# Modulation rows summed on VectorE, tables loaded behind the first weights, and two scores ahead of a norm

## The chip, the cores and the metric

The kernel runs on one core of one Trainium2 chip, in one launch. The metric is device microseconds of one execution; what is given for a kernel is the median of several runs.

## The reference

Two transformer-like blocks are computed one after the other, all in float32, for 512 tokens ("latent") and, in the first block, 256 context tokens beside them. What the change touches is this part of the first block (depth 2) and the attention of the second:

```python
for l in range(DEPTH):                                   # DEPTH = 2
    mod_l = jax.nn.silu(c) @ w_ada[l] + b_ada[l]         # w_ada: 1024 x 3072; c is one row
    sh_l, sc_l, gt_l = jnp.split(mod_l[:, None, :], 3, axis=-1)
    mod_c = jax.nn.silu(c_ctx) @ w_ada[l] + b_ada[l]     # the same for the context
    ...
    h_l = _rmsnorm(x, g_pre[l]) * (1.0 + sc_l) + sh_l
    pl = _split_proj(h_l @ w_in[l])                      # short conv, attention, gated linear attention
    ...
    x = x + gt_l * _rmsnorm(out_l, g_post[l])
# second block
bq = rms_norm(bq.reshape(B, S, B_HEADS, HEAD_DIM_2), gains[2])
cq = rms_norm(cq.reshape(B, S, C_HEADS, HEAD_DIM_2), gains[4])
oa = diff_attention(aq, ak, av, lam, bias_a)             # heads A, B and C
ob = banded_attention(bq, bk, bv, bias_b, B_WINDOW, sinks[layer])
oc = nsa_attention(cq, kc, vc, ksel, ckv[:, :, 3], kwin, ...)
```

A modulation row is a product of a vector of 1024 with a matrix: the two vectors silu(c) and silu(c_ctx) against each 128 columns of `w_ada`.

## The kernel before, in words

Every engine has its own instruction stream, written out by hand in the order in which it works; the streams meet at semaphores and, at the end of each phase, at a barrier (`phase_end`) that all of PE, ACT and DVE pass.

**A tile** is a weight block of 1024 x 128 floats (512 KB) in one of the four slots of `ring`. SP loads it in two DMAs of 256 KB (`load`, L638), in the order of use and not before the slot is free (`w_used`). POOL splits it in two halves of rounded numbers, `whi` and `ring_parts`, with two instructions of 128x1024 (`split`, L859 and L861). PE then multiplies (`turned_tile`, three matmuls for each of eight 128-row pieces and each stretch of tokens) into one of two PSUM pairs, used in turn; a pair is free again when ACT or DVE has read it (`pair_free`).

**The phases** are: load, ada0, then for each layer attn, branch1, gla, branch2, conv, branch0, and for the second block kv2, cmp, heads, branches2, up, down, end.

**Load and ada0.** SP issues the constants (`con`, 3008 KB in one DMA: identity, ones, two more matrices and a rotation in the first 640 columns; then cosines, sines and the tables of the linear attention), x (2048 KB), ctx (1024 KB) and 24 small rows (L643). PE, POOL and the rest wait until all have landed (`inputs_in`). PE transposes x, ACT copies it out, the phase ends; SP then writes x to DRAM (`keep_x`) and goes on with `w_ada`. In ada0 PE computes the squares' sums and then 16 modulation tiles of layer 0 as matmuls with 2 moving columns. The first four are loaded ahead.

**conv0** is the convolution phase of layer 0. It has eight iterations; one is four tiles of 768 tokens, in the order z, c, x, b. ACT takes the tanh of z (`z_tanh`) and copies c; DVE multiplies tanh and z (that frees the pair for x), multiplies c and x (frees it for the next z), runs seven instructions of the convolution on SBUF (L2402 and L2055) and multiplies with b. Between the tiles lie the 32 modulation tiles that are still needed (8 of layer 0, 24 of layer 1): SP loads one beside each ring tile into `mod_ring` (`load_mod`, L707), and PE, behind each of the four tiles, multiplies it in 8 matmuls with 2 moving columns. Each such fp32 matmul stands twice in the trace. DVE copies the 8 numbers of an iteration to `mods` (L2417).

**heads** starts with four query tiles, each followed by a norm (ACT squares, PE sums with `block_norm_mm`, ACT takes the root, DVE multiplies in `normed_query`). Then PE runs `scores`, with DVE's `maximum` (L2553), ACT's exp and DVE's `normalise` behind, 96 heads' pieces long. PE issues `all_read`, one small matmul for the gates, and waits for the fourth norm before the first score; ACT's fourth norm stands ahead of its first exp.

Of the kernel before, what the change touches and what calls it, by code (L numbers as in the profile page):

```python
# [22 lines left out]
P = 128  # L23
# [198 lines left out]
def two_blocks(nc, a, out, stop=None):  # L222
    ctx = ExitStack()
    with ctx:
# [3 lines left out]
        def sem(name):  # L228
            return ctx.enter_context(nc.semaphore(name))
# [49 lines left out]
        def take(*shape, at=None):  # L279

            n = int(np.prod(shape))
            o = used[0] if at is None else at
            used[0] = o + n
            assert used[0] <= FREE, (shape, used[0], FREE)
            v = arena[:, o:o + n]
            if len(shape) == 2:
                v = v.rearrange("p (a b) -> p a b", a=shape[0])
            if len(shape) == 3:
                v = v.rearrange("p (a b c) -> p a b c", a=shape[0], b=shape[1])
            return v  # L290
# [26 lines left out]

        mod_ring = take(4, KT, P, at=used[0] - KT * ALL)
        gin = arena[:, base:base + 4 * ALL].rearrange("p (s n) -> p s n", s=4)
# [137 lines left out]
        h_ready, h_scaled, h_hi, h_lo = sem("h_ready"), sem("h_scaled"), sem("h_hi"), sem("h_lo")  # L457
        mod_landed, mod_used = [sem(f"mod_landed{s}") for s in range(4)], sem("mod_used")
        x_kept, x_back, x_new = [sem(f"x_kept{h}") for h in range(2)], sem("x_back"), sem("x_new")
        pair_free = [sem(f"pair_free{s}") for s in range(2)]  # L460

        phase, inputs_in, out_done = sem("phase"), sem("inputs_in"), sem("out_done")
        act_own, dve_own = sem("act_own"), sem("dve_own")
        x_turned, par_turned = sem("x_turned"), sem("par_turned")
# [163 lines left out]
        def _(sp):  # L628
# [15 lines left out]

            sp.dma_start(con[:], a["con"]).then_inc(inputs_in, 16)
            sp.dma_start(y_in[:, 0:LT, :], a["x"][0].rearrange("(t p) f -> p t f", p=P)).then_inc(inputs_in, 16)
# [43 lines left out]
            for l in range(DEPTH):  # L690
                w = a["w_in"][l]
                n = ALL if l == 0 else LAT
                if l == 0:

                    for s in range(4):
                        load(a["w_ada"][0][:, s * P:(s + 1) * P])
                    sp.wait_ge(phase, 3 * phases_to("load"))
                    keep_x(ALL)
                    with sp.Fori(0, 3) as i, tiles.loop(i, 3, 4):
                        for s in range(4):  # L700
                            load(a["w_ada"][0][:, ds(i * 512 + (4 + s) * P, P)])
# [7 lines left out]
                def conv(i, mods_of=None):  # L709

                    for s, c in enumerate((CZ, CC, CX, CB)):
                        load(w[:, i * P + c:i * P + c + P] if isinstance(i, int) else w[:, ds(i * P + c, P)])
                        if mods_of:

                            if not isinstance(i, int) or i > 0:
                                sp.wait_ge(mod_used, i * 4 + (s - 3))
                            else:
                                sp.wait_ge(phase, 3 * phases_to("branch2_0"))
                            load_mod(s, mods_of(s))
# [43 lines left out]
                if l == 0:  # L763

                    for i in range(2):
                        conv(i, lambda s: a["w_ada"][0][:, (16 + 4 * i + s) * P:(17 + 4 * i + s) * P])
                    with sp.Fori(0, 6) as i, tiles.loop(i, 6, 4):
                        conv(i + 2, lambda s: a["w_ada"][1][:, ds(i * 512 + s * P, P)])
                else:
                    with sp.Fori(0, KT) as i, tiles.loop(i, KT, 4):  # L770
                        conv(i)
# [127 lines left out]
        def _(pe):  # L899
# [143 lines left out]
            for l in range(DEPTH):  # L1043
# [20 lines left out]

                def conv(i, cond):
                    for s in range(4):
                        turned_tile(hP, n)
                        if cond is None:
                            continue

                        pe.wait_ge(mod_landed[s], i * 32 + 32)
                        if s == 0:
                            pe.wait_ge(mod_read, i)
                        for k in range(KT):
                            last = mm(bank(6)[:, 2 * s:2 * s + 2], mod_ring[:, s, k], cond[:, :, k], k == 0, k == KT - 1)
                        last.then_inc(mod_used, 1)

# [226 lines left out]
                if phase_end(f"branch2_{l}"):  # L1304
                    return
                if l == 0:
                    with pe.Fori(0, 2) as i, tiles.loop(i, 2, 4), uses.loop(i, 2, 4), splits.loop(i, 2, 4):
                        conv(i, conds[0])
                    with pe.Fori(0, 6) as i, tiles.loop(i, 6, 4), uses.loop(i, 6, 4), splits.loop(i, 6, 4):
                        conv(i + 2, conds[1])  # L1310
                else:
                    with pe.Fori(0, KT) as i, tiles.loop(i, KT, 4), uses.loop(i, KT, 4), splits.loop(i, KT, 4):
                        conv(i, None)
                if phase_end(f"conv{l}"):
# [68 lines left out]
            for c in range(4):  # L1383
                turned_tile(hP, LAT)
                if c:
                    block_norm_mm(NORM0 + c - 1, blk)
            block_norm_mm(NORM0 + 3, blk)
            all_read()
            fill_steps = [0]
# [78 lines left out]
            mm(bank(1, 96), anti, gates.rearrange("p t m -> p (t m)"), True, True).then_inc(gates_turned, 1)  # L1468
            pe.wait_ge(n2_ready, NORM0 + 4)
            for n in range(3):  # L1470
                scores(n)
            for n in range(4 * NS2 + 3):
# [569 lines left out]
        def _(dve):  # L2042
# [79 lines left out]
            for l in range(DEPTH):  # L2122
# [52 lines left out]
                def rotated_tile(c, dst):  # L2175
                    dve.wait_ge(rot_read, c + 1)
                    dve.wait_ge(qn_ready, c + 1)
                    v.tensor_tensor(dst[:, 0:LAT], rope_t, rope_s, ALU.add).then_inc(q_ready, 1)

                nb = NORMED * l  # L2180
                qg, kg = par[l][:, R_QG:R_QG + 1], par[l][:, R_KG:R_KG + 1]
# [199 lines left out]
                ns = len(stretches)  # L2381
                with dve.Fori(0, KT) as i, tiles.loop(i, KT, 4), uses.loop(i, KT, 4), own.loop(i, KT, 4 * ns):
                    p = product()
                    dve.wait_ge(z_tanh, i + KT * l + 1)
                    last_read()
                    stt(tmp[:, 0:n], tha[:, 0:n], 1.0, pair(p, n), ALU.add, ALU.mult).then_inc(pair_free[p], 1)
                    skip()
                    last_read()
# [25 lines left out]
                    if l == 0:  # L2414

                        dve.wait_ge(mod_used, i * 4 + 4)
                        v.tensor_copy(mods[:, ds(i * 4 + 16, 4)], bank(6, 8).rearrange("p (a b) -> p a b", a=4)).then_inc(mod_read, 1)  # L2417
# [114 lines left out]
            own(v.tensor_scalar(nsink, sinkb, -1.0, None, ALU.mult))  # L2532
            for c, g in enumerate((0, 1, 2, 4)):
                normed_query(NORM0 + c, qt_[:, 0, c], gain(g), c)
# [57 lines left out]
            maximum(0)  # L2592
            maximum(1)
            for n in range(4 * NS2):
                i, m = divmod(n, NS2)
# [95 lines left out]
```

## Time and profile before

| | |
|---|---|
| median of 3 runs | 4250.06 us (4243.55 to 4252.66) |
| the profiled execution | 4246.85 us; span of the trace 4245.0 us |
| PE | 3942.7 us busy, 93% of the span, mean granted clock 0.955 |
| POOL | 1945.0 us, 46% |
| DVE | 1675.9 us, 39% |
| ACT | 974.7 us, 23% |
| DMA | 305.21 MB, mean 72 GB/s |

Times are microseconds from the start of the span. An engine's idle time costs something only if the work that ends last waits for it. A matmul's own duration overlaps with the next one's, so the distance from start to start is what counts.

### The profile page before, as it was taken

To read this page: it belongs to the slowest core of one execution; us is meant where nothing else is said; L and a number is where in the kernel's file an instruction comes from. 1 tells how busy PE (TensorE), PEld (TensorE's weight loads), DVE (VectorE), ACT (ScalarE), POOL (GpSimd) and SP (SyncE) were. 2 spreads that over 40 slices of the span, in tenths; PEclk is the share of its full clock that TensorE was granted. 3 is DMA by queue.
4 is the path that set the end of the run, shared out by engine and by line. 5 is a ranking of instruction groups with operands and counts; after the bars stand their busy time and mean duration, and the time that the engine had idled before them with its cause. 6 is when DMAs were issued, how large, how long until landed. Compare 5 with 4: busy or idle time off the path is not lost. (4 is left out here: it accounts for less than half of the span.)

```text
span 4245.0 us, 52930 instructions
## 1 busy us (share of the span) xinstructions
PE 3942.7 (93%) x20171; PEld 3147.9 (74%) x20171; DVE 1675.9 (39%) x2552; ACT 974.7 (23%) x1729; POOL 1945.0 (46%) x834
## 2 busy tenths in 40 slices
PE   6999999999989998899999998899888998999999
PEld 5777788888878897676678777677585544877877
DVE  1444317556631224244426555445303555132200
ACT  2333312222210001334312222110213444102200
POOL 1333243332335444344453433587452220886886
PEclk7899999999999998999999999999888998999999
DMA  6111221111226543222231221334432110343333
GB/s 189 41 46 46 61 68 46 47 43 46 52 64 127 106 89 109 70 48 60 56 82 49 60 55 45 82 93 100 120 90 55 33 35 8 92 106 79 94 92 91
DMA packets 512284, 305.21 MB, mean 72 GB/s; under 512 B 37769, under 2 KB 492818, under 8 KB 511210
## 3 DMA queue, kind: packets, MB, share of 16 engines
q1 hardware_dynamic: 500010, 282.43, 27.3%
q10 hardware_dynamic: 12096, 20.33, 1.4%
q8 instruction: 122, 2.00, 0.2%
q14 instruction: 56, 0.46, 0.0%
HBM read 276.42 MB, written 26.27 MB: 71 GB/s over the span
## 5 line engine op out<-in xcount | busy, mean ns | idle before, releaser
L859 POOL TENSOR_TENSOR whi<-ring,con 128x1024 fp32r<-128x1024 f32 (+1 forms) x415 | 967.4, 2331 | 2245.1 <-DMA ring<-in_w_in 1740.0
L548 PE MATMUL ps<-xT_parts,whi 128*128 128x512 f32 (+2 forms) x2632 | 1009.9, 384 | 63.0 <-DVE hT_parts L2093 35.7
L548 PE MATMUL ps<-hT_parts,whi 128*128 128x512 f32 (+1 forms) x2864 | 1049.8, 367 | 0.0
L861 POOL TENSOR_TENSOR ring_parts<-ring,whi 128x1024 fp32r<-128x1024 f32 (+1 forms) x415 | 979.5, 2360 | 32.5
L548 PE MATMUL ps<-xT_parts,ring_parts 128*128 128x512 f32 (+2 forms) x2600 | 945.6, 364 | 0.0
L548 PE MATMUL ps<-arena_parts,whi 128*128 128x512 f32 (+1 forms) x2472 | 767.7, 383 | 68.7 <-DVE arena_parts L2087 57.8
L1544 ACT ACTIVATE arena<-ps 128x512 f32<-128x512 f32 (+7 forms) x583 | 311.4, 544 | 1685.6 <-PE ps L548 975.1
L548 PE MATMUL ps<-arena 128*128 128x128 f32 (+9 forms) x3292 | 646.0, 341 | 27.6 <-DVE arena L2055 21.9
L548 PEld LDWEIGHTS ps<-xT_parts,whi 128*128 128x128 f32 (+1 forms) x2632 | 501.0, 190 | 170.2 <-issue 66.1
L548 PEld LDWEIGHTS ps<-hT_parts,whi 128*128 128x128 f32 x2864 | 544.9, 190 | 90.8 <-issue 7.0
L548 PEld LDWEIGHTS ps<-arena_parts,whi 128*128 128x128 f32 x2472 | 460.2, 194 | 177.2 <-issue 66.3
L548 PEld LDWEIGHTS ps<-arena 128*128 128x128 f32 (+3 forms) x3292 | 438.4, 194 | 180.5 <-issue 122.1
L548 PEld LDWEIGHTS ps<-xT_parts,ring_parts 128*128 128x128 f32 (+1 forms) x2600 | 492.9, 190 | 84.5 <-issue 0.8
L548 PE MATMUL ps<-arena_parts,ring_parts 128*128 128x512 f32 (+1 forms) x1440 | 549.5, 382 | 0.0
L2055 DVE SCALAR_TENSOR_TENSOR arena<-arena,ps 128x256 f32<-128x256 f32 (+2 forms) x200 | 127.6, 638 | 553.4 <-PE ps L548 417.8
L548 PEld LDWEIGHTS ps<-arena_parts,ring_parts 128*128 128x128 f32 x1440 | 278.9, 194 | 52.0
L548 PE MATMUL ps<-arena,con 128*128 128x512 f32 (+5 forms) x626 | 227.0, 501 | 29.2 <-ACT arena L1544 28.7
L548 PE MATMUL ps<-whi,xT_parts 128*128 128x256 f32 (+2 forms) x640 | 190.0, 297 | 10.8 <-ACT arena L1544 7.3
L548 PE MATMUL ps<-whi,hT_parts 128*128 128x256 f32 (+2 forms) x640 | 184.0, 287 | 0.0
L548 PE MATMUL ps<-ring_parts,xT_parts 128*128 128x256 f32 (+2 forms) x640 | 183.5, 287 | 0.0
L548 PEld LDWEIGHTS ps<-arena,con 128*128 128x128 f32 (+1 forms) x626 | 99.2, 177 | 109.2 <-issue 59.6
L2055 DVE SCALAR_TENSOR_TENSOR arena<-arena,par 128x512 f32<-128x512 f32 (+2 forms) x83 | 103.3, 1252 | 192.3 <-ACT arena L1544 185.7
(158 smaller groups left out, 3388.2 us busy)
## 6 DMA issues: line engine op xcount, KB each, us to landing
ring<-in_w_in SPq DMA_DIRECT2D x504, 256.0 KB, 3.9
arena<-in_w_ada SPq DMA_DIRECT2D x64, 256.0 KB, 4.8
ring<-in_w_up SPq DMA_DIRECT2D x64, 256.0 KB, 4.0
ring<-in_w_down SPq DMA_DIRECT2D x64, 256.0 KB, 3.9
ring<-in_w_out SPq DMA_DIRECT2D x48, 256.0 KB, 3.8
gates_kept<-stage ACTq DMA_DIRECT2D x24, 384.0 KB, 3.9
arena<-gates_kept SPq DMA_DIRECT2D x24, 384.0 KB, 3.7
ring<-in_w_ada SPq DMA_DIRECT2D x32, 256.0 KB, 4.0
```

The source lines that it names most:

```text
L548: return nc.tensor.matmul(o, l, r, start=first, stop=last)
L859: v.tensor_tensor(hi, raw, ones[:, 0:m].unsqueeze(1).to_broadcast([P, kt, m]), ALU.mult).then_inc(w_rounded, 1)
L861: v.tensor_tensor(ringR[:, s, 0:kt, 0:m], raw, hi.bitcast(F32), ALU.subtract).then_inc(w_split, 1)
L1544: return nc.scalar.activation(o, i, f, **kw)
L2055: return v.scalar_tensor_tensor(out=o, in0=a0, scalar=s, in1=a1, op0=op0, op1=op1)
```

## The change

There are three parts.

**Modulation rows in conv0.** A slot of `mod_ring` now holds 256 rows by 512 columns of `w_ada` (two pieces of 128 rows; runs of 2 KB in DRAM, before 512 bytes) and the four slots hold all 1024 rows. DVE weighs: for each of the eight pieces k and each of the two vectors c it multiplies the piece with the vector's numbers, one per partition, and adds it to `mod_sum[:, c]` (128x512): 16 instructions in an iteration, eight ahead of the product of z and eight behind it, with a wait for the own last ones ahead of each k. Then it raises `mod_summed`. PE sums over the partitions with ones as the moving operand: 8 matmuls with one column in an iteration, behind tile b, instead of 32. SP waits for `mod_summed` of the iteration before ahead of every slot, where before it waited for PE's use of that slot. `conds[1]`, which holds the same numbers as `conds[0]`, serves both layers.

**Constants in two DMAs.** The first 640 columns go first as before; the rest (5376 columns, 2688 KB) goes behind the first four tiles of `w_ada`, and ahead of SP's wait for the phase and of `keep_x`. DVE waits for it (`tables_in`) ahead of its first use.

**Heads.** PE issues the gates' matmul and the first two scores behind the third norm's matmul, then `all_read`, the fourth norm's matmul, the third score, and a wait for the fourth root. DVE takes the gates and the first two maxima ahead of the fourth `normed_query`.

```diff
-        mod_ring = take(4, KT, P, at=used[0] - KT * ALL)
+        mod_ring = take(4, 2, 512, at=used[0] - KT * ALL)
+        mod_sum = take(2, 512)
+        used[0] += KT * ALL - 5 * 1024
...
-            sp.dma_start(con[:], a["con"]).then_inc(inputs_in, 16)
+            first_con = C_AT["cos"][0]
+            sp.dma_start(con[:, 0:first_con], a["con"][:, 0:first_con]).then_inc(inputs_in, 16)
...
                     for s in range(4):
                         load(a["w_ada"][0][:, s * P:(s + 1) * P])
+                    sp.dma_start(con[:, first_con:], a["con"][:, first_con:]).then_inc(tables_in, 16)
                     sp.wait_ge(phase, 3 * phases_to("load"))
                     keep_x(ALL)
...
                             if not isinstance(i, int) or i > 0:
-                                sp.wait_ge(mod_used, i * 4 + (s - 3))
+                                sp.wait_ge(mod_summed, i)
...
-                        conv(i, lambda s: a["w_ada"][0][:, (16 + 4 * i + s) * P:(17 + 4 * i + s) * P])
+                        conv(i, lambda s: a["w_ada"][0][256 * s:256 * s + 256, (16 + 4 * i) * P:(20 + 4 * i) * P])
...
-                def conv(i, cond):
+                def conv(i, with_mods):
                     for s in range(4):
                         turned_tile(hP, n)
-                        if cond is None:
-                            continue
-
-                        pe.wait_ge(mod_landed[s], i * 32 + 32)
-                        if s == 0:
+                        if s == 3 and with_mods:
+                            pe.wait_ge(mod_summed, i + 1)
                             pe.wait_ge(mod_read, i)
-                        for k in range(KT):
-                            last = mm(bank(6)[:, 2 * s:2 * s + 2], mod_ring[:, s, k], cond[:, :, k], k == 0, k == KT - 1)
-                        last.then_inc(mod_used, 1)
+                            for m in range(4):
+                                for c in range(2):
+                                    last = mm(bank(6)[:, 2 * m + c:2 * m + c + 1], mod_sum[:, c, m * P:(m + 1) * P],
+                                              ones[:, 0:1], True, True)
+                            last.then_inc(mod_used, 1)
...
-            block_norm_mm(NORM0 + 3, blk)
-            all_read()
...
-            pe.wait_ge(n2_ready, NORM0 + 4)
-            for n in range(3):
-                scores(n)
+            scores(0)
+            scores(1)
+            all_read()
+            block_norm_mm(NORM0 + 3, blk)
+            scores(2)
+            pe.wait_ge(rs2_ready, NORM0 + 4)
...
+                dve.wait_ge(tables_in, 16)
...
+                def weigh_mods(i, ks):
+
+                    for k in ks:
+                        if k % 2 == 0:
+                            dve.wait_ge(mod_landed[k // 2], i * 32 + 32)
+                        own.settle()
+                        for c in range(2):
+                            m_, c_ = mod_ring[:, k // 2, k % 2], conds[1][:, c, k:k + 1]
+                            if k == 0:
+                                own(v.tensor_scalar(mod_sum[:, c], m_, c_, None, ALU.mult))
+                            else:
+                                own(stt(mod_sum[:, c], m_, c_, mod_sum[:, c], ALU.mult, ALU.add))
+
+                with dve.Fori(0, KT) as i, tiles.loop(i, KT, 4), uses.loop(i, KT, 4), own.loop(i, KT, 4 * ns + 16 * (l == 0)):
+                    if l == 0:
+                        weigh_mods(i, range(4))
                     p = product()
                     dve.wait_ge(z_tanh, i + KT * l + 1)
                     last_read()
                     stt(tmp[:, 0:n], tha[:, 0:n], 1.0, pair(p, n), ALU.add, ALU.mult).then_inc(pair_free[p], 1)
+                    if l == 0:
+                        weigh_mods(i, range(4, KT))
+                        own.settle()
+                        v.memset(stat[:, 3, 6:7], 0.0).then_inc(mod_summed, 1)
...
-                        dve.wait_ge(mod_used, i * 4 + 4)
+                        dve.wait_ge(mod_used, i + 1)
...
-            for c, g in enumerate((0, 1, 2, 4)):
+            for c, g in enumerate((0, 1, 2)):
                 normed_query(NORM0 + c, qt_[:, 0, c], gain(g), c)
...
             maximum(0)
             maximum(1)
+            normed_query(NORM0 + 3, qt_[:, 0, 3], gain(4), 3)
```

## Rows read from the trace of the kernel before

**Rows 1.** The page, part 1: busy time, share of the span, instructions.
```profile
PE 3942.7 (93%) x20171; PEld 3147.9 (74%) x20171; DVE 1675.9 (39%) x2552; ACT 974.7 (23%) x1729; POOL 1945.0 (46%) x834
```

**Rows 2.** Busy time by stretch, conv0: us, busy (count) of each, clock, DMA.
```profile
1360.00:1400.00 40.00, 40.00 (x255) 35.93 (x254) 7.46 (x12) 2.90 (x3) 19.30 (x8) 1.00 0.50 101
```

**Rows 3.** Timeline of PE, start of conv0: start, us, operation, count, idle before.
```profile
1274.56 0.49 PE L548 MATMUL ps<-xT_parts,whi 128*128 128x512 f32 x1 [2.36 <-DVEq L2049]
...
1276.17 0.63 PE L548 MATMUL ps<-xT_parts,whi 128*128 128x512 f32 x1
...
1284.59 1.84 PE L548 MATMUL ps<-small,arena 128*128 128x2 f32 x16
1286.93 0.49 PE L548 MATMUL ps<-xT_parts,whi 128*128 128x512 f32 x1 [0.50 <-POOL ring_parts L861]
...
1295.44 1.84 PE L548 MATMUL ps<-small,arena 128*128 128x2 f32 x16
1297.14 0.48 PE L548 MATMUL ps<-xT_parts,whi 128*128 128x512 f32 x1
```

**Rows 4.** Timeline of DVE, conv0, the third iteration and the fourth's first product.
```profile
1369.07 0.95 DVE L2055 SCALAR_TENSOR_TENSOR arena<-arena,ps 128x768 f32<-128x768 f32 x1 [10.51 <-ACT arena L1544]
1387.16 1.15 DVE L2393 TENSOR_TENSOR arena<-arena,ps 128x512 f32<-128x512 f32 x2 [17.14 <-PE ps L548]
1388.46 0.49 DVE L2402 TENSOR_SCALAR arena<-arena,par 128x512 f32<-128x512 f32 x1 [0.15 <-DVE arena L2393]
1389.11 0.75 DVE L2055 SCALAR_TENSOR_TENSOR arena<-arena,par 128x512 f32<-128x512 f32 x1 [0.16 <-DVE arena L2402]
1390.01 0.75 DVE L2055 SCALAR_TENSOR_TENSOR arena<-arena,par 128x512 f32<-128x512 f32 x1 [0.15 <-DVE arena L2055]
1390.80 0.35 DVE L2402 TENSOR_SCALAR arena<-arena,par 128x256 f32<-128x256 f32 x1
...
1392.23 0.96 DVE L2055 SCALAR_TENSOR_TENSOR arena<-arena 128x768 f32<-128x768 f32 x1
...
1409.71 0.95 DVE L2055 SCALAR_TENSOR_TENSOR arena<-arena,ps 128x768 f32<-128x768 f32 x1 [10.51 <-ACT arena L1544]
```

**Rows 5.** Timeline of DVE, conv0, the convolution's last instruction one iteration later.
```profile
1432.86 3.13 DVE L2055 SCALAR_TENSOR_TENSOR arena<-arena 128x768 f32<-128x768 f32 x1
```

**Rows 6.** Timeline of POOL, the same moment.
```profile
1432.78 2.40 POOL L859 TENSOR_TENSOR whi<-ring,con 128x1024 fp32r<-128x1024 f32 x1 [5.31 <-DMA ring<-in_w_in]
1435.26 2.99 POOL L861 TENSOR_TENSOR ring_parts<-ring,whi 128x1024 fp32r<-128x1024 f32 x1
```

**Rows 7.** Timeline of DVE, the same convolution in layer 1, where POOL hardly rests.
```profile
2754.47 2.65 DVE L2055 SCALAR_TENSOR_TENSOR arena<-arena,par 128x512 f32<-128x512 f32 x1 [0.16 <-DVE arena L2402]
2757.63 2.38 DVE L2055 SCALAR_TENSOR_TENSOR arena<-arena,par 128x512 f32<-128x512 f32 x1 [0.51 <-DVE arena L2055]
```

**Rows 8.** Timeline of SP's queue, conv0: the issue of one ring tile.
```profile
1326.28 1.42 SPq L638 DMA_DIRECT2D ring<-in_w_in  x2
```

**Rows 9.** Timeline of POOL, the start on that tile.
```profile
1331.28 2.41 POOL L859 TENSOR_TENSOR whi<-ring,con 128x1024 fp32r<-128x1024 f32 x1 [5.63 <-DMA ring<-in_w_in]
```

**Rows 10.** Timeline of the start: SP's last small row and PE's first work.
```profile
12.73 0.34 SPq L643 DMA_DIRECT2D arena<-in_norm_mlp  x1
...
22.87 0.85 PE L1022 MATMUL ps<-con,arena 108*128 108x108 f32 x3 [22.87 <-DMA arena<-in_norm_mlp]
```

**Rows 11.** Busy time by stretch: the first loads, and ada0 behind its third tile.
```profile
0.00:22.80 22.80, 0.00 (x0) 0.00 (x0) 0.09 (x2) 1.28 (x1) 0.20 (x4) 1.00 0.96 318
...
50.50:60.00 9.50, 9.50 (x46) 9.50 (x46) 0.48 (x3) 0.00 (x0) 0.00 (x0) 0.50 1.02 205
```

**Rows 12.** Timeline of DVE, ada0: the copies behind the third and the fourth tile.
```profile
50.62 0.16 DVE L2141 COPY mods<-ps 128x2 f32 x1 [1.63 <-PE ps L548]
53.89 0.16 DVE L2141 COPY mods<-ps 128x2 f32 x1 [3.12 <-PE ps L548]
```

**Rows 13.** Timelines of PE, DVE and ACT at the first scores.
```profile
3229.07 1.13 PE L548 MATMUL ps<-arena,con 128*128 128x512 f32 x2 [1.93 <-ACT arena L1544]
...
3233.93 1.72 PE L548 MATMUL ps<-arena 64*128 64x128 f32 x8 [2.63 <-DVE arena L2055]
...
3232.00 1.88 DVE L2055 SCALAR_TENSOR_TENSOR arena<-arena,par 128x512 f32<-128x512 f32 x1 [1.90 <-ACT arena L1544]
...
3230.13 0.60 ACT L1544 ACTIVATE arena<-ps 128x512 f32<-128x512 f32 x1 [1.11 <-DVE arena L2055]
```

More of the change, by code:

```diff
@@ L458, in two_blocks @@
         mod_landed, mod_used = [sem(f"mod_landed{s}") for s in range(4)], sem("mod_used")
+        mod_summed = sem("mod_summed")
         x_kept, x_back, x_new = [sem(f"x_kept{h}") for h in range(2)], sem("x_back"), sem("x_new")
@@ L462, in two_blocks @@
         phase, inputs_in, out_done = sem("phase"), sem("inputs_in"), sem("out_done")
+        tables_in = sem("tables_in")
         act_own, dve_own = sem("act_own"), sem("dve_own")
@@ L765, in _ @@
                     for i in range(2):
-                        conv(i, lambda s: a["w_ada"][0][:, (16 + 4 * i + s) * P:(17 + 4 * i + s) * P])
+                        conv(i, lambda s: a["w_ada"][0][256 * s:256 * s + 256, (16 + 4 * i) * P:(20 + 4 * i) * P])
                     with sp.Fori(0, 6) as i, tiles.loop(i, 6, 4):
-                        conv(i + 2, lambda s: a["w_ada"][1][:, ds(i * 512 + s * P, P)])
+                        conv(i + 2, lambda s: a["w_ada"][1][256 * s:256 * s + 256, ds(i * 512, 512)])
                 else:
@@ L1305, in _ @@
                     return
[L1306 to L1313, printed above, removed]
+                with pe.Fori(0, KT) as i, tiles.loop(i, KT, 4), uses.loop(i, KT, 4), splits.loop(i, KT, 4):
+                    conv(i, l == 0)
                 if phase_end(f"conv{l}"):
@@ L2381, in _ @@
                 ns = len(stretches)
-                with dve.Fori(0, KT) as i, tiles.loop(i, KT, 4), uses.loop(i, KT, 4), own.loop(i, KT, 4 * ns):
+                def weigh_mods(i, ks):
[12 more added lines that the diff above has]
+                        weigh_mods(i, range(4))
                     p = product()
```

## Prediction

> **What bounds the kernel now.** I read the page first: PE is busy 93% of the span, POOL 46%, DVE 39% [rows 1], so time is won where PE gets less to do or waits less, and lost where another engine takes over. Then the busy time by stretch for the stages that the change touches. In conv0 PE is busy 40.00 of 40 us at full clock, while POOL works 19.30 us and DVE 7.46 [rows 2]: PE sets the pace there, and DVE looks nearly empty. The timelines tell the rest. On PE's, the 16 records (8 matmuls) of a modulation tile hold the next tile back from 1295.44 to 1297.14, so 1.70 us [rows 3]. On DVE's, the product of z comes every 40.64 us (1369.07 to 1409.71), the length of an iteration [rows 4]. An iteration is four tiles and four times 1.70, so a bare tile is (40.64 - 6.80) / 4 = 8.46 us. At the start nothing computes for 22.87 us until the inputs have landed, with the DMA engines 0.96 busy at 318 GB/s [rows 10, 11]. At the first scores PE waits 2.63 us for DVE's fourth norm [rows 13].
>
> **Part 1, conv0, what PE saves.** 32 matmuls with 2 columns become 8 with one: three of four stretches of 1.70 us go, 5.10 us an iteration. The trace has no one-column matmul; its nearest row is the two-column one, whose length is set by loading weights, so I take 1.70 for eight of them (from 1.5 to 2.0). If PE stays the pace, an iteration is 35.54 us and eight save 40.8 us.
>
> **What DVE gets.** 16 instructions of 128x512 with all operands in SBUF. With POOL silent such a one starts 0.79 us after the one before it (1390.01 to 1390.80), or 0.90 with the wait for its own result (1389.11 to 1390.01) [rows 4]. Two per k: 1.69 us, less for k = 0, so 6.3 us for the eight ahead of z's product and 6.8 for the eight behind. That is 13 us beside some 9 us of old work: by busy time alone it fits into 35.5 us easily.
>
> **Why it fits badly.** DVE's instructions on SBUF and POOL's splits exclude each other. The convolution's last instruction takes 0.96 us with POOL silent [rows 4] and 3.13 when it starts just after a split [rows 5]: it ends 0.81 us after that split does, and the next split grows from 2.40 to 2.99 [rows 6]. In layer 1, where POOL hardly rests, the 0.75 us instruction takes 2.65 and 2.38, one per split [rows 7]. So each split that meets a stream of such instructions costs the stream 1.6 to 2.2 us (2.65 - 0.75 = 1.90, 3.13 - 0.96 = 2.17), at most a whole split, 2.4 [rows 6]; I take 2.1. Products that read PSUM are not held up: 0.95 each time [rows 4].
>
> The Trainium skill, SBUF — State Buffer, "Who interferes with whom", has this as a rule that speaks against the change: a VectorE instruction with two SBUF inputs and a GpSimd instruction that reads SBUF shut each other out for the whole instruction, whichever starts first. The rows agree with it (3.13 against 0.96). By that rule at its hardest, each meeting costing a whole split of 2.40 us, the loop worked out next would be 23.1 + 8 x 2.40 = 42.3 us, against the 38.9 that I take.
>
> **The loop that closes on DVE.** The pair that z used must be freed before tile x may start. From z's product to the next one: tile x 8.46; product c times x 1.30; seven instructions of the convolution 4.73 (1388.46 to 1393.19) [rows 4]; b's product and the copy about 1.3; the eight weighings ahead of z 6.3; z's product 1.0. Sum 23.1 us without POOL. The second eight weighings lie under tile x.
>
> POOL adds eight splits an iteration. How many fall into the 15 exposed instructions? SP decides. Its mod slots, and behind them the ring tiles c, x and b, now wait for `mod_summed`, which comes only near the end of tile x. A ring tile reaches POOL 5.0 us after issue (1326.28 to 1331.28) [rows 8, 9]. So c and x are split when the convolution runs, b and the next z during the first weighings: nearly all eight splits hit the exposed stream. Seven give 23.1 + 14.7 = 37.8 us, eight give 39.9. I take the middle, 38.9. Tile x then waits for 38.9 - 35.5 = 3.4 us, and such a pause costs clock: behind the 2.36 us pause at 1274.56 matmuls come at half clock from 1276.17 on, seven of them at twice the distance, some 1.4 us [rows 3]. Taken in about a third of the iterations: 39.3 us. Bounds: 35.5 (no meeting that matters) and 23.1 + 8 x 2.4 + 1.4 = 43.7.
>
> So conv0 gains 8 x (40.64 - 39.3) = 10.7 us. At the end the last convolution, stretched by three splits (4.73 + 6.3 + 1.3 against a tile b of 8.46), ends late by 3.9 us less what overlaps: I take 3 back. **Net 8 us** (from +40 gained to 27 lost).
>
> What else moves there: the new mod DMAs have runs of 2 KB. The 512-byte runs go at 205 GB/s with the DMA engines full, the start's long ones at 318 [rows 11]; 4 MB in 39 us needs 108 GB/s either way, so this is nothing on the path. PE's new wait for `mod_summed` stands behind tile b, 8 us after the sum is made; behind it are queued only the sums and the next z. SP's wait holds back three ring tiles, by up to 7 us of the 25 us lead that four slots give: it costs nothing itself except that it bunches the splits.
>
> **Part 2, the constants.** Ahead of the first work 6080 KB become 3392. At 318 GB/s this takes 11 us instead of 19.6. But SP issues its last small row only at 12.73 [rows 10], and small ones need some 2 us to land: start at about 15.2 instead of 22.87, 7.7 us earlier. What is late next: SP's queue. Behind the four `w_ada` tiles (2 MB at 205 GB/s [rows 11], until 24) come 2688 KB of tables (until 32.5), then `keep_x`'s 3 MB (until 42), and only then the fifth tile, here at about 46. PE's third tile ends at 50.6 before, so at 42.9 now, and a tile takes 1.8 us there (1.63 idle and 0.16 between DVE's copies) [rows 12]: it would want the fifth tile at 44.7. Behind it the clock is 0.50 and a tile takes 3.4 us, twice 1.70, slower than DMA's 2.6 (512 KB at 205 GB/s) [rows 11], so nothing more is lost. 1.3 us back, rounded: **6.5 us gained** (3 to 8; if the row issue went faster, too).
>
> **Part 3, the heads.** The first scores leave the 2.63 us wait behind [rows 13], but `all_read` now stands ahead of the fourth norm's matmul and waits for ACT's copy that ends at 3230.73, where the matmul had started at 3229.07: the fourth root, and ACT's first exp queued behind it, come 1.6 us later. Maxima 0 and 1 are saved on DVE. I take 0.5 us gained, from 1.5 gained to 1.5 lost, the loss if the norm meets a split once more.
>
> **Sum.** 8 + 6.5 + 0.5 = 15 us off the profiled execution, 4246.85 - 15 = 4231.9. It lies 3.2 us under the median shown, so the forecast for a median is 4235.
>
> **Rivals.**
> A, the forecast: DVE and POOL in turn set conv0's pace, 38 to 40.3 us; 4235 (4228 to 4244).
> B, PE keeps the pace: the loads land so that most splits fall under tile x or where DVE waits for PE, 35.5 to 37.5 us an iteration. For it: DVE's busy time is small [rows 2]; against it: SP's order. 25 to 40 us in conv0, 4203 to 4218, middle 4211.
> C, slower: all eight splits meet the exposed stream at 2.2 to 2.4 us and the clock falls at each pause. It loses in all from 41.1 us an iteration on, since the two other parts' 7 us less 3 at the end are then used up; at 42.6 us it is 15.7 + 3 - 7 = 12 us slower, 4262.
> D, the start gives nothing: the tables only push `keep_x` and the fifth tile, and PE waits there for what it had won; conv0 as in A. 4241. The DMA row (0.96 busy) speaks for it; that the copies from the third tile on come 3.3 us apart [rows 12], more than DMA's 2.6 for a tile, against it.
>
> **Chances.** A 0.56, B 0.20, C 0.14, D 0.10. A measurement of this kernel tells about 0.2%, 8.5 us, from no change. A is beyond that in four of five cases (0.45), D in less than half (0.04), B always: faster 0.69. C lies beyond it with 0.08, the rest is the same, 0.23. For the range I leave out the lower half of B and the upper half of C: 4212 to 4255.
>
> **What would show it.** In the changed trace: PE's records of 128x1 in eight places, 1.7 us each; z's product every 39 us (B: 35.5; C: over 41); weighings of 0.75 us beside ones of 2.4 to 2.7, one per split; a pause of PE ahead of tile x put down to DVE, and the clock under 1.00 in conv0, where it was 1.00; PE's first matmul at 15 us; ada0's fifth tile late by about 1 us and all that follows ada0 some 6 us earlier. Wrong would be the forecast if weighings that meet splits don't stretch, if the splits fall elsewhere, or if the fifth tile of `w_ada` waits long.

## The result

The changed kernel takes 4226.6 us (median of 13 runs, 4210.3 to 4240.5) where the kernel before takes 4251.3 us (13 runs, 4243.6 to 4268.3) beside it. The ratio is 0.9938, 95% interval 0.9922 to 0.9953: 20 to 33 us faster. The profiled execution of after has a span of 4225.5 us, 19.5 less than before's.

The page of after, part 1, to be laid beside [rows 1]:

```profile
PE 3915.8 (93%) x19787; PEld 3111.2 (74%) x19787; DVE 1858.1 (44%) x2688; ACT 975.5 (23%) x1729; POOL 1958.6 (46%) x834
```

PE has 384 records fewer (8 iterations, 24 matmuls, two records each) and DVE 136 instructions more: 8 times 16 weighings and a memset.

**conv0.** Busy time by stretch of after (the columns of [rows 2]), around its second and third iteration:

```profile
1300.00:1340.00 40.00, 33.21 (x189) 28.97 (x188) 35.71 (x32) 2.91 (x3) 21.12 (x8) 0.91 0.56 112
1340.00:1380.00 40.00, 40.00 (x236) 35.15 (x235) 35.52 (x34) 2.91 (x3) 20.69 (x8) 1.00 0.54 114
```

DVE, 7.46 us in [rows 2], is busy for 35.5 of 40. PE has lost 6.79 us of the first stretch and nothing of the second. The timeline of after's DVE, from one product of z (1286.67) over the next (1330.34) to the third (1365.06):

```profile
1286.67 0.94 DVE L2055 SCALAR_TENSOR_TENSOR arena<-arena,ps 128x768 f32<-128x768 f32 x1
1287.54 13.37 DVE L2055 SCALAR_TENSOR_TENSOR arena<-arena,cond 128x512 f32<-128x512 f32 x8
...
1301.13 1.15 DVE L2413 TENSOR_TENSOR arena<-arena,ps 128x512 f32<-128x512 f32 x2
...
1306.20 0.96 DVE L2055 SCALAR_TENSOR_TENSOR arena<-arena 128x768 f32<-128x768 f32 x1
...
1308.48 5.20 DVE L2392 TENSOR_SCALAR arena<-arena,cond 128x512 f32<-128x512 f32 x2
1313.71 16.71 DVE L2055 SCALAR_TENSOR_TENSOR arena<-arena,cond 128x512 f32<-128x512 f32 x6
1330.34 0.94 DVE L2055 SCALAR_TENSOR_TENSOR arena<-arena,ps 128x768 f32<-128x768 f32 x1
1331.21 5.75 DVE L2055 SCALAR_TENSOR_TENSOR arena<-arena,cond 128x512 f32<-128x512 f32 x8
1337.03 0.06 DVE L2406 MEMSET stat<- 128x1 f32 x1
1341.49 1.15 DVE L2413 TENSOR_TENSOR arena<-arena,ps 128x512 f32<-128x512 f32 x2 [4.40 <-PE ps L552]
...
1345.13 2.38 DVE L2422 TENSOR_SCALAR arena<-arena,par 128x256 f32<-128x256 f32 x1
...
1352.66 3.04 DVE L2055 SCALAR_TENSOR_TENSOR arena<-arena 128x768 f32<-128x768 f32 x1
...
1356.80 4.00 DVE L2392 TENSOR_SCALAR arena<-arena,cond 128x512 f32<-128x512 f32 x2
1360.83 4.32 DVE L2055 SCALAR_TENSOR_TENSOR arena<-arena,cond 128x512 f32<-128x512 f32 x6
1365.06 0.95 DVE L2055 SCALAR_TENSOR_TENSOR arena<-arena,ps 128x768 f32<-128x768 f32 x1
```

And POOL's at the same time, the first and the last of eight splits without a rest, and the next one:

```profile
1308.44 2.41 POOL L865 TENSOR_TENSOR whi<-ring,con 128x1024 fp32r<-128x1024 f32 x1 [10.98 <-DMA ring<-in_w_in]
...
1327.20 2.67 POOL L867 TENSOR_TENSOR ring_parts<-ring,whi 128x1024 fp32r<-128x1024 f32 x1
1344.58 2.79 POOL L865 TENSOR_TENSOR whi<-ring,con 128x1024 fp32r<-128x1024 f32 x1 [14.71 <-DMA ring<-in_w_in]
```

The first iteration lasts 43.67 us, the second 34.72. In the first all eight splits meet the eight weighings ahead of z: 5.20 + 16.71 = 21.9 us, where the same number with POOL silent (1331.21) takes 5.75, so 2.0 us per split. Four more splits had met the weighings behind z before (13.37 instead of 5.75 us), so that the product of c and x came 14.46 us after z's: twelve splits met in one interval. In the second POOL rests until the convolution has begun; the eight weighings behind z stand untouched, DVE waits 4.40 us for PE, and six splits meet what it has to do until z. Long iterations don't follow each other: the intervals between products of z are 43.67, 34.72, 36.02, 40.19, 34.97, 38.10, 36.09, mean 37.7, where before each was 40.64. What PE sees of it, timeline and waits of after in conv0 (for the waits: us in total, times, longest):

```profile
1305.94 1.84 PE L552 MATMUL ps<-con,arena 128*128 128x1 f32 x16
1307.64 0.47 PE L552 MATMUL ps<-xT_parts,whi 128*128 128x512 f32 x1
...
1331.43 0.77 PE L552 MATMUL ps<-xT_parts,whi 128*128 128x512 f32 x1 [6.79 <-DVE arena L2055]
```
```profile
PE ps L552 <- DVE arena L2055: 11.5, 4, 6.8
```

From DVE's first instruction in conv0 to the last copy of modulation numbers the phase takes 305.5 us, before 327.9: 22.4 us less.

**The start.** SP's last small row and PE's first work, after's answer to [rows 10]:

```profile
10.32 0.29 SPq L647 DMA_DIRECT2D arena<-in_norm_mlp  x1
...
16.38 0.85 PE L1028 MATMUL ps<-con,arena 108*128 108x108 f32 x3 [16.38 <-DMA arena<-in_norm_mlp]
```

PE starts 6.49 us earlier. DVE's copies of ada0, which answer to [rows 12], follow each other as before: the fourth comes 3.24 us behind the third (3.27 there), and the fifth 3.42 behind the fourth (57.31 - 53.89 = 3.42 there), so the fifth tile isn't late:

```profile
44.14 0.16 DVE L2141 COPY mods<-ps 128x2 f32 x1 [1.63 <-PE ps L552]
47.38 0.16 DVE L2141 COPY mods<-ps 128x2 f32 x1 [3.09 <-PE ps L552]
50.80 0.16 DVE L2141 COPY mods<-ps 128x2 f32 x1 [3.25 <-PE ps L552]
```

**Where the rest went.** At the start of conv0 after is 6.2 us ahead of before, at its end 28.6, at the first product of branch0 31.2, at the first norm of heads 30.5 (3215.74 against 3185.27), at the 51st of DVE's 160 maxima there 29.9, at the 121st 29.2, at the last only 19.4. Those last 10 us are lost in one place. Busy time by stretch, after from 3512 on and then before at the same point of its work, 29 us later (the column behind POOL's is the granted clock):

```profile
3512.00:3522.00 10.00, 9.67 (x22) 4.04 (x21) 5.33 (x19) 5.47 (x18) 0.00 (x0) 0.50 0.01 2
3522.00:3532.00 10.00, 10.00 (x30) 5.58 (x28) 2.37 (x8) 2.11 (x6) 0.00 (x0) 0.50 0.00 0
3532.00:3542.00 10.00, 9.86 (x33) 6.50 (x32) 5.95 (x28) 4.47 (x18) 0.00 (x0) 0.50 0.00 1
```
```profile
3541.00:3551.00 10.00, 9.10 (x40) 4.67 (x40) 7.20 (x27) 6.96 (x24) 0.00 (x0) 1.00 0.00 1
3551.00:3561.00 10.00, 8.81 (x45) 5.53 (x44) 6.96 (x32) 5.50 (x21) 0.00 (x0) 0.92 0.01 2
3561.00:3571.00 10.00, 10.00 (x19) 3.09 (x17) 3.42 (x14) 2.73 (x9) 0.00 (x0) 0.57 0.00 1
```

In after PE works for 30 us at the lower of its two levels, 1.2 GHz, and gets less done; before is there at 2.4 GHz for nearly all of the first two stretches. Whether the change causes it is a question for a second trace.

### The profile page after: what moved, and what is told of

It reads as the page before. It is cut to its first block and busy times, and to the rows that moved or that the text cites. A ratio compares the mean times of both kernels' runs of the same rounds, so it can differ in the third digit from the quotient of the medians.

```text
span 4225.5 us, 52354 instructions
## 1 busy us (share of the span) xinstructions
PE 3915.8 (93%) x19787; PEld 3111.2 (74%) x19787; DVE 1858.1 (44%) x2688; ACT 975.5 (23%) x1729; POOL 1958.6 (46%) x834
## 5 line engine op out<-in xcount | busy, mean ns | idle before, releaser
L865 POOL TENSOR_TENSOR whi<-ring,con 128x1024 fp32r<-128x1024 f32 (+1 forms) x415 | 977.3, 2355 | 2211.7 <-DMA ring<-in_w_in 1714.0
L552 PE MATMUL ps<-xT_parts,whi 128*128 128x512 f32 (+2 forms) x2632 | 1010.0, 384 | 77.0 <-DVE hT_parts L2093 36.1
L867 POOL TENSOR_TENSOR ring_parts<-ring,whi 128x1024 fp32r<-128x1024 f32 (+1 forms) x415 | 983.7, 2370 | 32.5
L552 PE MATMUL ps<-arena 128*128 128x128 f32 (+9 forms) x3292 | 655.6, 343 | 25.2 <-DVE arena L2055 19.4
L552 PE MATMUL ps<-arena,con 128*128 128x512 f32 (+6 forms) x626 | 231.0, 509 | 28.9 <-ACT arena L1544 28.5
```

The lines of the kernel that those rows point to most:

```text
L552: return nc.tensor.matmul(o, l, r, start=first, stop=last)
L865: v.tensor_tensor(hi, raw, ones[:, 0:m].unsqueeze(1).to_broadcast([P, kt, m]), ALU.mult).then_inc(w_rounded, 1)
L867: v.tensor_tensor(ringR[:, s, 0:kt, 0:m], raw, hi.bitcast(F32), ALU.subtract).then_inc(w_split, 1)
```

## The experiments

**One part at a time.** The first three kernels hold one part of the change each, the other two taken back.

> The kernel before with the modulation rows on VectorE alone; the constants in one DMA and the heads' order as before. Theory P (the gain is made in conv0, where DVE and POOL take turns): nearly all of the gain is here. The product of z comes every 37.7 us on average, as in the changed kernel's trace (34.7 to 43.7), conv0 is shorter by 22 us, and the median lies 15 to 25 us under the kernel before. Rival S (the gain is mostly the start's): under 10 us faster, because what conv0 wins is given back at the phase's end.

Measured: 4225.6 us, ratio 0.9945 (0.9932 to 0.9959), 23.6 us under the 4249.2 of before. Its conv0 takes 304.3 us, intervals of 33.9 to 41.5, and PE waits for DVE five times, 10.0 us in all. Nearly the whole gain is this part's.

> The kernel before with the constants in two DMAs alone. Theory P: PE starts at 16.4 instead of 22.9 us and the fifth tile of w_ada is not late, so 6 us faster, 4 to 8. Rival D (the tables push keep_x and the fifth tile): PE starts at 16.4 but the fourth and fifth modulation tiles are more than 3.4 us apart, and 0 to 3 us are left. Rival S: 12 us or more.

Measured: 4244.9 us, 0.9989 (0.9979 to 0.9998), 4.3 us less (1 to 9 by the interval, which only just leaves out no change). PE's first work is at 16.31, 6.56 us earlier, and conv0 starts 4.5 us earlier, as was expected. It is the trace more than the time that shows this part's gain.

> The kernel before with the new order at the first scores alone. Theory P: the first scores start some 5 us earlier, but the fourth norm is later, so the third maximum comes 0 to 3 us earlier and the time is the same, within 3 us. Rival H (the new order shifts TensorE's clock in the heads phase): slower by 5 to 12 us, with a stretch of over 30 us at the lower clock behind 3500 us, as in the changed kernel's trace.

Measured: 4249.4 us, 1.0002 (0.9993 to 1.0012). Nothing. In after the first two maxima are 35.3 us ahead of before, the third to tenth 32.5 to 32.3, and from the twelfth to the sixtieth 29.9 to 30.2, a little less than the 30.5 that the phase came in with. The scores overtake the norm, and within a dozen maxima the lead is given back. Two things take it. Here, in heads_only, which comes in 1.7 us behind before, the first two maxima are 3.0 us ahead and the third 2.0 behind, for its fourth norm starts just after a split of POOL (at 3234.84) and takes 2.79 us; in after it takes 0.80 (at 3202.38):

```profile
3234.95 2.79 DVE L2056 SCALAR_TENSOR_TENSOR arena<-arena,par 128x512 f32<-128x512 f32 x1 [2.59 <-ACT arena L1545]
```

In after the 2.0 us that are left at the third maximum go ahead of the twelfth, where PE is still at 1.2 GHz (granted clock 0.50 from 3223.5 to 3227.5) at the point of its work at which before was at 2.4 GHz again (1.00 from 3256 to 3260). That the new order shifts the clock there is not shown: one trace of each was compared.

The ratios multiply to 0.9945 x 0.9989 x 1.0002 = 0.9936; the whole change has 0.9938. Within the 5 us or so that such a product can tell, the parts don't disturb each other.

**Less to weigh.** Eight weighings an iteration instead of 16 (two ahead of z, six behind), so that the modulation rows lack half of their sum:

```diff
-                        weigh_mods(i, range(4))
+                        weigh_mods(i, range(1))
...
-                        weigh_mods(i, range(4, KT))
+                        weigh_mods(i, (2, 4, 6))
```

> The changed kernel with half of the weighings left out: DVE weighs the pieces 0, 2, 4 and 6 only (2 instructions ahead of z's product and 6 behind, of 16), so the modulation rows lack half of their sum. All loads and waits stay. Theory P (DVE's stream, shut out by POOL's splits, holds tile x back): the stream ahead of z's product is 2 instructions long, so tile x never waits, z's product comes every 35.5 us and conv0 ends 15 to 19 us earlier than in the changed kernel; median 4205 to 4215. Rival L (PE waits because ring tiles are loaded late behind the wait for mod_summed): conv0 loses at most 5 us, PE's idle time is put down to POOL, not to DVE.

Measured: 4208.2 us, 0.9904 (0.9874 to 0.9934), conv0 286.4 us. From the second iteration on each takes 35.3 us, and PE waits for DVE nowhere in the loop. Two rows of its DVE:

```profile
1360.87 0.95 DVE L2055 SCALAR_TENSOR_TENSOR arena<-arena,ps 128x768 f32<-128x768 f32 x1 [1.55 <-ACT arena L1544]
...
1375.40 1.14 DVE L2413 TENSOR_TENSOR arena<-arena,ps 128x512 f32<-128x512 f32 x2 [5.07 <-PE ps L552]
```

Both products wait for what PE made: PE is the pace again. So what after loses against PE's pace is DVE's weighing, 19.1 us of conv0 (15 to 19 expected), and not the loads or the one-column sums, which are the same here.

**The order of the weighings.** All 16 behind z's product, none ahead of it:

```diff
-                        weigh_mods(i, range(4))
...
-                        weigh_mods(i, range(4, KT))
+                        weigh_mods(i, range(KT))
```

> The changed kernel with all 16 weighings behind z's product, none ahead. Theory P: z's product is no longer held back; the 16 weighings (13 us alone, up to 8 splits of 2.1 us among them) lie under tile c's rest and tile x, 13.5 us, so the product of c and x may come late and hold back the next z instead: 35.5 to 38 us an iteration, 0 to 15 us faster than the changed kernel in conv0. Rival L: no difference to the changed kernel, within 3 us, or slower, since mod_summed comes later.

Measured: 4230.3 us, 0.9955 (0.9939 to 0.9971); intervals 36.2 to 37.3, more even than after's, as expected, and 1.1 us shorter on average (36.6 against 37.7), but no gain: conv0 takes 311.1 us, 5.6 more than after's. The phase's end eats it. The last iteration of this kernel, DVE, and PE's sums that wait for it:

```profile
1545.42 3.02 DVE L2392 TENSOR_SCALAR arena<-arena,cond 128x512 f32<-128x512 f32 x2
1548.48 30.80 DVE L2055 SCALAR_TENSOR_TENSOR arena<-arena,cond 128x512 f32<-128x512 f32 x14
```
```profile
1579.45 3.58 PE L552 MATMUL ps<-con,arena 128*128 128x1 f32 x16 [10.78 <-DVE stat L2404]
```

The last 16 weighings take 33.8 us instead of 11.5, for POOL goes on with the tiles ahead of it, the next phase's too (eleven splits start in that time, 2.0 us each), and PE stands 10.8 us.

**The order of the loads.** If the place of the splits is what costs, SP's order should change it. In after SP issues ring tile z, waits for `mod_summed`, loads slot 0, and only then issues c, x and b, with a slot behind each. Here ring tile c goes ahead of the wait, and slots 0 and 1 come together behind it:

```diff
-                        if mods_of:
+                        if mods_of and s:
...
+                            if s == 1:
+                                load_mod(0, mods_of(0))
                             load_mod(s, mods_of(s))
```

> The changed kernel with SP's order changed: ring tiles z and c are issued ahead of the first wait for mod_summed, and both first mod slots behind it. Theory P (this order bunches the splits into the exposed stream): tile c's two splits move under the weighings behind z's product, so two splits less, about 4 us, hit the exposed stream in the long iterations; the iteration is 36 to 37 us on average and conv0 5 to 12 us shorter. Rival L: as much, but with PE's idle time put down to POOL in the changed kernel. Rival N (SP's order does not matter): the same within 3 us.

Measured: 4206.9 us (4202.9 to 4211.2), 0.9901 (0.9885 to 0.9918); intervals 39.15, 35.04, 35.06, 35.04, 35.06, 32.45, 38.04; conv0 288.8 us, 16.7 less than after's, with all 16 weighings, and more than the 5 to 12 expected. An iteration of its DVE:

```profile
1344.28 0.96 DVE L2059 SCALAR_TENSOR_TENSOR arena<-arena 128x768 f32<-128x768 f32 x1
...
1346.33 0.87 DVE L2396 TENSOR_SCALAR arena<-arena,cond 128x512 f32<-128x512 f32 x2
1347.23 10.64 DVE L2059 SCALAR_TENSOR_TENSOR arena<-arena,cond 128x512 f32<-128x512 f32 x6
1357.79 0.94 DVE L2059 SCALAR_TENSOR_TENSOR arena<-arena,ps 128x768 f32<-128x768 f32 x1
1358.66 15.38 DVE L2059 SCALAR_TENSOR_TENSOR arena<-arena,cond 128x512 f32<-128x512 f32 x8
...
1374.26 1.15 DVE L2417 TENSOR_TENSOR arena<-arena,ps 128x512 f32<-128x512 f32 x2
```

and of its POOL, the first and the last split of eight:

```profile
1348.98 2.71 POOL L869 TENSOR_TENSOR whi<-ring,con 128x1024 fp32r<-128x1024 f32 x1 [12.65 <-DMA ring<-in_w_in]
...
1368.65 2.73 POOL L871 TENSOR_TENSOR ring_parts<-ring,whi 128x1024 fp32r<-128x1024 f32 x1
```

The splits still come in one bunch and all eight are still met: the weighings ahead of z take 11.5 us, those behind it 15.4, together 15.4 more than the 11.5 they take with POOL silent, 1.9 a split. But the bunch lies across z's product, in the same place each time, and the convolution is over before it (0.96 us for its last instruction). So DVE has 19.7 us of its own and 15.4 for eight splits, 35.05 in all, in four of seven intervals, waiting for nothing but its own results. PE's own pace is 35.30: that far apart are its one-column sums in this kernel (1412.14, 1447.44, 1482.74) as in few_weighed. DVE is just below it, and PE waits for DVE nowhere in the loop. (The intervals 32.45 and 38.04 make 70.5 together, twice PE's pace; what parted them was not looked into.) After has the same amounts, but twelve splits in one interval and six in the next, and what DVE idles in the short one (4.40 us) is missing in the long one.

**Both orders together.** The two best guesses in one kernel.

> Both: rings z and c ahead of the wait, and all 16 weighings behind z's product. Theory P: the best or as good as the better one of the two; 35.5 to 36.5 us an iteration, conv0 10 to 17 us shorter than in the changed kernel, median 4207 to 4217. If mod_summed comes too late for the mod loads, the next weighings wait for DMA, which shows as DVE idle time put down to in_w_ada.

Measured: 4237.0 us, 0.9975 (0.9964 to 0.9986), the slowest of the kernels that weigh all 16: the expectation failed. The intervals are 35.3 to 41.3 us, conv0 takes 321.6. Its DVE, and what PE waits for in conv0:

```profile
1401.53 0.95 DVE L2059 SCALAR_TENSOR_TENSOR arena<-arena,ps 128x768 f32<-128x768 f32 x1 [7.11 <-ACT arena L1548]
1402.40 4.75 DVE L2396 TENSOR_SCALAR arena<-arena,cond 128x512 f32<-128x512 f32 x2
1407.18 18.62 DVE L2059 SCALAR_TENSOR_TENSOR arena<-arena,cond 128x512 f32<-128x512 f32 x14
...
1426.03 1.15 DVE L2415 TENSOR_TENSOR arena<-arena,ps 128x512 f32<-128x512 f32 x2
```
```profile
PE ps L552 <- DVE stat L2408: 17.2, 5, 7.8
```

I had counted everything behind z's product as hidden. It is hidden only until PE comes to the one-column sums behind tile b, which wait for `mod_summed`: 22.8 us after z's product here (1401.53 to 1424.3, where PE begins to idle; the sums start at 1425.99). The 16 weighings and the splits among them take until 1425.9, 24.3 us after it, and while PE waits for them its next z waits too; ahead of z's product DVE idles 7.1 us. In the loop the sums come 38.1 to 38.8 us apart, every time within 0.2 us of `mod_summed`. In all_behind the same 16 end 23.0 us after z's product (1398.22 to 1421.24) and PE comes to the sums at 24.6 (1422.84): there it fits by 1.6 us. Cover has a length. The loads, which the expectation feared, are not what is late: DVE waits for no weight in the loop. Half ahead and half behind, as the change has it, with the splits across the middle, fits both covers.

**Again, side by side.** Two questions were left: whether the stretch at 1.2 GHz belongs to after, and whether 20 us between after and rings_first come from different runs.

> The changed kernel once more, word for word, beside the two that follow. In its first profiled execution TensorE's granted clock stayed at 0.50 for 37.5 us from 3515.7 on, and the distance to the kernel before shrank from about 29 us to 19 there. Theory E: that stretch belongs to the execution, not to the kernel. The second trace has only pieces of 10 us there, the convolution is again some 305 us long (304 to 308) with long and short iterations by turns, and the span is 27 to 31 us under that of the kernel before. Rival K: it belongs to the kernel (the new order of the heads): the same stretch stands there again and the span is 18 to 21 us under that of before. Median about 4225 either way.

Measured: 4218.4 us, 0.9918 (0.9903 to 0.9932); span 4216.5, 28.5 under before. Its conv0 is 301.6 us long, a little less than expected, with intervals of 41.6, 36.0, 37.9, 33.9, 38.0, 36.1 and 36.1 us (mean 37.1): the long first one is there again, the order of the others is not. At the place in question stands:

```profile
3512.00:3522.00 10.00, 9.05 (x40) 4.76 (x40) 7.35 (x27) 7.10 (x25) 0.00 (x0) 1.00 0.00 1
3522.00:3532.00 10.00, 8.84 (x46) 5.54 (x44) 6.96 (x32) 5.38 (x21) 0.00 (x0) 0.93 0.00 1
3532.00:3542.00 10.00, 10.00 (x18) 2.99 (x17) 3.29 (x14) 2.85 (x10) 0.00 (x0) 0.56 0.01 2
```

The long stretch isn't there: it belongs to the one execution. But this execution shows another such thing: it is 41.2 us ahead at the third maximum in heads and 29.7 at the 32nd. At that third maximum after and after_again, one kernel, lie 8.7 us apart, and at the 32nd 0.2.

> The ring tiles ahead of the modulation slots, as before, now measured on the same chip as the changed kernel. Theory P (the place where the splits fall decides): 14 to 20 us under the changed kernel by the medians, as the convolution is 289 against 305 us long, with iterations of 35.0 us. Rival V: the distance between the two earlier medians (4206.9 and 4226.6) came from chips and executions: 0 to 6 us, and long iterations turn up here too.

Measured: 4204.0 us, 0.9889 (0.9874 to 0.9905), 14.3 us under after_again on the same chip. Six of its seven intervals are 35.0 to 35.3, one 38.75; conv0 288.9 us. That meets the expectation (14 to 20) at its edge. The order of the loads is worth 13 to 17 us by the traces of conv0 (301.6 - 288.9 and 305.5 - 288.8) and 14 by these medians, and this kernel beats both others.

**The small rows.** What holds PE until 16.1 to 16.4 us (the last row is issued at 10.2 to 10.3)? The function `rows` and its calls moved word for word from SP's stream to the head of ACT's:

```diff
-                sp.dma_start(dst[r:r + n, c0:c0 + w], src).then_inc(inputs_in, 16)
...
+                act.dma_start(dst[r:r + n, c0:c0 + w], src).then_inc(inputs_in, 16)
```

> As rings_first, but ACT issues the 25 small rows from its own queue while SP issues the constants, x, ctx and then at once the first four tiles of w_ada. It asks what holds PE's first work at 16.1 to 16.4 us. Theory T: the last small row, issued by SP at 10.3 and landed 5.8 us later behind the large transfers of the same queue. Then the last row is issued at about 8.5 and lands soon, x and ctx are in at about 13.5 (3392 KB at 318 GB/s are 10.9 us, and 2 to 3 for the way), and PE starts at 13.5 to 14.5, 2 us earlier; median 2 us under rings_first_again, too little to be told apart by time, so the trace decides. Rival U: the rows are held back by the amount of data in all queues, and with 2 MB of w_ada issued earlier they land later: PE starts at 16 to 20.

Measured: 4203.7 us, 0.9889 (0.9874 to 0.9904): nothing by time. Its trace:

```profile
9.84 0.41 ACTq L1520 DMA_DIRECT2D arena<-in_norm_mlp  x1
...
16.95 0.85 PE L1007 MATMUL ps<-con,arena 108*128 108x108 f32 x3 [16.95 <-DMA arena<-in_norm_mlp]
```

ACT issues the last row hardly earlier than SP did (9.84 against 10.32 in after), and PE starts later than in rings_first (16.12). That the large transfers of the same queue hold the rows up falls; that the data of `w_ada`, issued earlier here, do so fits, but was not taken apart.

## Why the prediction was right, and where it was off

The median of 4226.6 us lies in the range (4212 to 4255) and on the side forecast, 8 us under 4235. It lies between the times of A, the forecast (4228 to 4244), and of its rival B (4203 to 4218): the mechanism was A's, but its largest term, conv0, was put at a third of what it is, and that the number still falls in the range is owed to the range's width. By its own steps:

**What PE saves: right.** Eight one-column matmuls take 1.70 us (1305.94 to 1307.64 in after, as the two-column ones in [rows 3]). PE's own pace was put at 35.54 us; the kernels where PE never waits in the loop show 35.30, so 5.34 us an iteration were saved and not 5.10.

**The price of a meeting: right.** 2.1 us per split was taken from [rows 5 to 7]; eight meetings cost 21.9 - 5.75 = 16.2 us, 2.0 each. The Trainium skill, SBUF — State Buffer, "Who interferes with whom", says that each side shuts the other out for a whole instruction; the rows agree (3.04 us at 1352.66 in after, beside a split, for the instruction that takes 0.96 at 1306.20), with 2.0 on the mean rather than 2.40.

**How many meet the exposed stream: the step that was mis-sized.** The prediction let seven to eight of eight splits hit what is exposed, in every iteration alike, and got 38.9, with the clock 39.3 us. The long iteration of after is worse than that: 14.46 + 7.35 (from the product of c and x to the first weighing) + 21.86 = 43.67 us. The upper bound, 43.7, was made of other terms, since the 3.3 us by which the weighings behind z end late had been counted as hidden under tile x. But a long iteration isn't followed by another. It leaves POOL ahead of its work and idle for 14.71 us (DMA, the next ring tile, ends the wait); the next weighings run in 5.75 us, `mod_summed` comes 6.7 us after z's product instead of 14.3, the interval has six splits instead of twelve, and PE paces it. The mean is 37.7 us, so eight iterations gain 23.5 us instead of 10.7. From the first iteration's one-column sums on PE to the eighth's (1305.94 to 1568.35) pass 262.4 us, of which 7 x 35.30 = 247.1 are PE's own; of the 15.3 above it 11.5 are the four waits for DVE, and most of the other 3.8 is clock: the iteration with the wait of 6.79 us is 1.6 longer than wait and pace together, that with 3.48 us 1.8 (the granted clock is 0.64 and 0.72 in the 6 us in which they end, 1330 to 1336 and 1442 to 1448). Such a pause was priced at 1.4, so that was right too; taken in a third of the iterations, it came in two of seven. few_weighed (no loss with half the weighings) shows that it is DVE's stream that PE waits for, and rings_first (no loss with all, the splits elsewhere) that the splits' place decides. The prediction's A and B were cases for the whole loop; that the loop could go between them, iteration by iteration, was not among the rivals.

**The end of the phase: too dear.** 3 us were to be given back. The phase shows 22.4 us gained against 23.5 by the intervals, 1.1 back, and the next phase's first product comes another 2.6 us earlier (eight DVE instructions ahead of it, L2087, take 8.09 us where before they took 11.39). In all conv0 is worth 25 us in the traces of before and after and 23.6 by conv_only's medians, not 8.

**The start: about right, by two errors.** PE was to start at 15.2; it starts at 16.38, because the last row, now issued at 10.32 and not 12.73, lets PE start 6.1 us later and not 2. In return the 1.3 us for a late fifth tile are not lost. Forecast 6.5, 6.2 in the trace at the start of conv0, 4.3 by start_only's medians (interval 1 to 9).

**Heads: right in size.** Forecast 0.5, bounds ±1.5; measured nothing, with an interval from 3 us faster to 5 slower. The loss that was named, a norm that meets a split, came in heads_only (2.79 us) and not in after (0.80), which gives its lead back where PE is still at 1.2 GHz.

**The sum.** 15 us forecast; the terms measured make 25 + 6 + 0 = 31 in the profiled execution, of which 29 still stand late in heads. Its span shows 19.5, since the stretch at 1.2 GHz took 10; the medians show 24.7. Had only the span been read, the forecast would have looked closer than it was.

## What to carry to other kernels

When work is put on VectorE beside GpSimd's, count not how many instructions meet, but which of them have someone waiting: a meeting costs some 2 us either way, and the order in which the loads are issued decides whether it lies on the path. Don't extend one iteration's placement to the whole loop: a stall changes where the next splits fall, and long and short iterations come by turns, so that the mean lies between two of the cases. And measure the length of the cover: what was hidden with eight instructions wasn't with sixteen.

## What the runs showed that was not expected

- One ring tile issued ahead of a wait in SP's queue instead of behind it was worth 13 to 17 us, more than half of what the change itself brings (25).
- Where POOL hardly rests (the last iteration of all_behind), 16 VectorE instructions of 0.72 us (5.75 / 8) take 33.8 us, 2.0 more for each of eleven splits.
- A TENSOR_SCALAR of 128x256, with one tensor in SBUF, is shut out like those with two: 0.35 us with POOL silent, 2.38 beside a split.
- Two traces of one kernel differ by 9 us in span; one of them has 30 us in a row at 1.2 GHz (3512 to 3542) where the other changes level, with the same kernel in both.
- PE's first work, which waits for the last small row, comes 6.1 us after that row's issue on SP's queue and 7.1 us after it on ACT's.
